# Raw token rows with their scale as a last column feed the expert gather, staged outside the tenth weight slot, whose load is asked for at the start of the phase

## The reference

```
xt      = rms_norm(h, norm_m[layer])                 # x * 1/sqrt(mean(x*x) + eps) * gain
group   = argmax softmax(xt @ w_rg + b_rg)           # 1 of 4 groups
experts = top 2 of the 8 experts of that group       # from xt @ w_re + b_re
hid     = silu(xt @ w_gate[e]) * (xt @ w_up[e])      # 1024 -> 512, for each chosen expert
h       = h + sum over the 2 experts of gate * (hid @ w_down[e])
```

## Time and profile before

| | us |
|---|---|
| runs, median of 3 | 1522.3 |
| the profiled execution, its own time | 1519.33 |
| its span in the profile | 1517.4 |
| TensorE busy | 1470.7 (97%) |
| VectorE busy | 634.6 (42%) |
| ScalarE busy | 285.0 (19%) |
| GpSimd busy | 73.0 (5%) |
| moved by DMA | 484.54 MB |

### The profile page before, as it was taken

The page is one execution under the profiler, slowest core; times in us unless marked ns, Lnnn a source line. Parts: engine busy times, 40 slices in busy tenths (PEclk is TensorE's granted clock), DMA queues, the critical chain, the costliest instruction groups (busy, mean ns, idle before and its releaser), DMA issues. The chain is left out here.

```text
span 1517.4 us, 20326 instructions
## 1 busy us (share of the span) xinstructions
PE 1470.7 (97%) x7727; PEld 738.4 (49%) x7727; DVE 634.6 (42%) x1657; ACT 285.0 (19%) x746; POOL 73.0 (5%) x123
## 2 busy tenths in 40 slices
PE   9999999999999999999999998899999999999995
PEld 8787878667333333333334445657333333333331
DVE  3666566445323323224244235735232322433324
ACT  2424244214110101001001004523010100110101
POOL 0101010001000000000000000001000000000000
PEclk9999999999999999999999999999999999999998
DMA  7432324467999999999999036785999999999993
GB/s 232 137 116 75 116 78 143 187 230 308 417 430 431 428 429 433 430 428 426 426 427 368 19 126 257 268 343 204 412 429 431 430 429 431 431 430 426 427 426 157
DMA packets 101504, 484.54 MB, mean 319 GB/s; under 512 B 16410, under 2 KB 51134, under 8 KB 67634
## 3 DMA queue, kind: packets, MB, share of 16 engines
q1 hardware_dynamic: 96818, 478.90, 78.0%
q0 software_dynamic: 4320, 4.42, 0.8%
q10 hardware_dynamic: 288, 0.14, 0.0%
HBM read 483.77 MB, written 10.97 MB: 326 GB/s over the span
## 5 line engine op out<-in xcount | busy, mean ns | idle before, releaser
L2539 PE MATMUL moe_ps_gate<-slots,moe_xrT 128*64 128x512 f32 x1024 | 228.1, 596 | 8.5 <-DMA slots<-in_w_gate_e_dram 8.5
L2539 PE MATMUL moe_ps_up<-slots,moe_xrT 128*64 128x512 f32 x1024 | 226.8, 595 | 0.0
L2566 PE MATMUL moe_ps_y<-slots,router_inputs 128*64 128x512 f32 x960 | 212.6, 595 | 0.0
L2412 DVE TENSOR_TENSOR resid<-resid,moe_ps_x 128x512 f32<-128x512 f32 x60 | 41.3, 688 | 252.7 <-PE moe_ps_x L2582 252.7
L2539 PEld LDWEIGHTS moe_ps_up<-slots,moe_xrT 128*64 128x64 f32 x1024 | 71.2, 137 | 150.9 <-issue 138.7
L2539 PEld LDWEIGHTS moe_ps_gate<-slots,moe_xrT 128*64 128x64 f32 x1024 | 72.2, 137 | 137.9 <-issue 136.7
L966 PE MATMUL gdn_bank<-gdn_xT,slots 128*128 128x288 f32 x512 | 136.3, 410 | 0.7 <-ACT slots L485 0.7
L2566 PEld LDWEIGHTS moe_ps_y<-slots,router_inputs 128*64 128x64 f32 x960 | 66.3, 137 | 124.9 <-issue 124.6
L2203 ACT ACTIVATE moe_xrT<-moe_ps_x,router_inputs 128x128 f32<-128x128 f32 x128 | 36.5, 367 | 379.1 <-PE moe_ps_x L2520 363.5
L966 PEld LDWEIGHTS gdn_bank<-gdn_xT,slots 128*128 128x128 f32 x512 | 92.6, 190 | 22.8 <-issue 1.1
L2381 DVE TENSOR_TENSOR router_inputs<-router_inputs,moe_ps_up 128x512 f32<-128x512 f32 x32 | 22.0, 688 | 195.0 <-PE moe_ps_up L2539 195.0
(11 more groups left out here) (509 smaller groups left out, 1817.9 us busy)
## 6 DMA issues: line engine op xcount, KB each, us to landing
slots<-in_w_gate_e_dram SPq DMA_DIRECT2D x40, 2048.0 KB, 23.0
slots<-in_w_up_e_dram SPq DMA_DIRECT2D x40, 2048.0 KB, 22.8
slots<-in_w_down_e_dram SPq DMA_DIRECT2D x40, 2048.0 KB, 25.8
slots<-in_w_gate_e_dram SPq DMA_DIRECT2D x48, 1024.0 KB, 26.2
slots<-in_w_up_e_dram SPq DMA_DIRECT2D x48, 1024.0 KB, 26.6
slots<-in_w_down_e_dram SPq DMA_DIRECT2D x48, 1024.0 KB, 26.0
slots<-in_w_in_a_dram SPq DMA_DIRECT2D x16, 1024.0 KB, 5.8
slots<-in_w_kv_dram SPq DMA_DIRECT2D x4, 2048.0 KB, 20.6
```

Source lines behind the costliest of these rows:

```text
L2412: V.tensor_tensor(half, half, banks[i][:, :], ALU.add).then_inc(s["summed"], 1)
L2539: last = T.matmul(ps[64 * e:64 * e + 64, :], xgT[:, k, 64 * e:64 * e + 64], slots[:, slot[2 * n + e], 512 * k:512 * k + 512], start=(k == ...
L2566: last = T.matmul(ps_y[64 * e:64 * e + 64, h, :], hidT[:, k, 64 * e:64 * e + 64], slots[:, slot[4 + e], 1024 * k + 512 * h:1024 * k + 512 ...
```

## The change

Rows are no longer normalised ahead of the gather. ACT reorders the raw rows into three buffers outside the slots: `norm_b`, `y_sb` and, for the 32 sample rows, the first 1024 columns of `xrT`, the last only after the logits have been made. SP stores them to `x_rows` in HBM, whose rows have 1025 numbers, and then stores `rstd` as the last column with three further DMAs. A gather brings 1025 numbers a row; GpSimd waits for it at once and copies the last column to `rcur` after the product of the group before. The scale is applied later: in `silu` as its `scale`, and in DVE's product with the up half, which becomes a `scalar_tensor_tensor`. For group 0 the scale goes into `sel0`, whose building instruction gets a second operation. The tail of the sample tile needs no clearing, since TensorE reads 32 rows of it. Piece 9 is the first DMA of the phase in layer 0, and follows pieces 4 and 5 in layer 1. ACT, DVE, GpSimd and SP wait for all six stores (`xn_stored` at 96) before the buffers are written again. The core of the diff:

```diff
@@ memory
-        sb("late_slots", [128, SLOT_COUNT - 7, SLOT_COLS])
-        xn = sb("last_slot", [128, SLOT_COLS])[:, 0:NT * D_MODEL].rearrange("p (t d) -> p t d", t=NT)
+        sb("late_slots", [128, SLOT_COUNT - 6, SLOT_COLS])
+        low = sb("low", [128, SLOTS])
+        rcur = sb("rcur", [128, 1])
...
+        xg_row = xr_flat[:, 0:D_MODEL + 1]
+        sel0 = xr_flat[:, 1544:1544 + NT * 128].rearrange("p (t r) -> p t r", t=NT)
+        x_rows = [norm_b[:, :], y_sb[:, :], xr_flat[0:T_DEC, 0:D_MODEL]]
@@ SP
             if layer:
                 m["prefetch"](sp, layer, (4, 5))
+            m["prefetch"](sp, layer, (9,))
             for t in range(NT):
-                sp.wait_ge(s["normed"], t + 1)
-                sp.dma_start(xn_dram[128 * t:128 * t + rows[t], :], xn[0:rows[t], t, :]).then_inc(s["xn_stored"], 16)
+                sp.wait_ge(s["turned_rows"], t + 1)
+                sp.dma_start(x_dram[128 * t:128 * t + rows[t], 0:D_MODEL], x_rows[t]).then_inc(s["xn_stored"], 16)
+            sp.wait_ge(s["inverse"], 1)
+            for t in range(NT):
+                sp.dma_start(x_dram[128 * t:128 * t + rows[t], D_MODEL:D_MODEL + 1], rstd[0:rows[t], t:t + 1], allow_slow_non_contiguous=True).then_inc(s["xn_stored"], 16)
             if layer == 0:
                 m["attn_inputs"](sp)
-            sp.wait_ge(s["xn_stored"], 16 * NT)
-            sp.wait_ge(s["gx_T"], 1)
-            m["prefetch"](sp, layer, (9,))
+            sp.wait_ge(s["xn_stored"], 16 * 2 * NT)
@@ POOL
-            P.memset(xn[32:64, 2, :], 0.0).then_inc(s["tail_cleared"], 1)
-            pool.wait_ge(s["tail_cleared"], 1)
-            P.memset(xn[64:128, 2, :], 0.0).then_inc(s["tail_cleared"], 1)
-            pool.wait_ge(s["tail_cleared"], 2)
-            pool.wait_ge(s["logits_made"], NT)
-            P.memset(xg, 0.0).then_inc(s["cleared"], 1)
+            pool.wait_ge(s["xn_stored"], 16 * 2 * NT)
+            pool.wait_ge(s["gx_T"], 1)
+            P.memset(xg_row, 0.0).then_inc(s["cleared"], 1)
...
+                pool.wait_ge(s["gathered"], n * 16)
+                pool.wait_ge(s["hidden"], n)
+                pool.sem_inc(s["waits_held"], 1)
+                P.tensor_copy(rcur[:, :], xg_row[:, D_MODEL:D_MODEL + 1]).then_inc(s["r_kept"], 1)
@@ ACT
-            act.wait_ge(s["inverse"], 1)
             for t in range(NT):
-                A.activation(by_tile(xn[0:r, t, :]), strided(resid[0:r, t, :]), ACT.Copy, scale=rstd[0:r, t:t + 1]).then_inc(s["normed"], 1)
+                if t == 2:
+                    act.wait_ge(s["logits_made"], NT)
+                A.copy(by_tile(x_rows[t]), strided(resid[0:rows[t], t, :])).then_inc(s["turned_rows"], 1)
...
+                    act.wait_ge(s["r_kept"], g)
+                    A.activation(hid, ps_gate[:], ACT.Silu, scale=rcur[:, 0:1]).then_inc(s["silued"], 1)
...
+            act.wait_ge(s["xn_stored"], 16 * 2 * NT)
             rows_kept(0)
             silu(0)
@@ DVE
-                    last = V.tensor_scalar(sel0[:, t, SLOTS * e:SLOTS * e + SLOTS], low, pos0[:, t, e:e + 1], None, ALU.is_equal)
+                    last = V.tensor_scalar(sel0[:, t, SLOTS * e:SLOTS * e + SLOTS], low[:, :], pos0[:, t, e:e + 1], rstd[:, t:t + 1], ALU.is_equal, ALU.mult)
...
+                    V.scalar_tensor_tensor(hid, hid, rcur[:, 0:1], ps_up[:], ALU.mult, ALU.mult).then_inc(s["hidden"], 1)
...
+            dve.wait_ge(s["xn_stored"], 16 * 2 * NT)
             overflow()
@@ PE
-            pe.wait_ge(s["normed"], NT)
-            pe.wait_ge(s["tail_cleared"], 2)
+            pe.wait_ge(s["turned_rows"], NT)
...
-                    last = T.matmul(ps_x[:, k // 4, k % 4, :], by_tile(xn[:, t, :])[:, k, :], sel0[:, t, :], start=(t == 0), stop=(t == NT - 1))
+                    last = T.matmul(ps_x[:, k // 4, k % 4, :], by_tile(x_rows[t])[:, k, :], sel0[0:rows[t], t, :], start=(t == 0), stop=(t == NT - 1))
```

More of the change, by code:

```diff
@@ L2007, in moe_phase @@
         place_o = y_sb[:, 0:TOP_K * NT * 128].rearrange("p (k t r) -> p k t r", k=TOP_K, t=NT)
[L2008 to L2009 removed]
         BELOW = -1024.0
         xr_flat = xrT[:].rearrange("p k r -> p (k r)")
[L2012 to L2014 removed]
+        xg_row = xr_flat[:, 0:D_MODEL + 1]
+        xg = xr_flat[:, 0:D_MODEL]
+        xgT = xr_flat[:, 1032:2056].rearrange("p (k r) -> p k r", k=KT)
+        obf = y_sb[0:1, 768:768 + 2 * OVER_GROUPS * N_EXPERTS].rearrange("p (b e) -> p b e", e=N_EXPERTS)
         selT = w_router.rearrange("p k n -> p (k n)")[:, 0:T_ALL]
+        sel0 = xr_flat[:, 1544:1544 + NT * 128].rearrange("p (t r) -> p t r", t=NT)
+        x_rows = [norm_b[:, :], y_sb[:, :], xr_flat[0:T_DEC, 0:D_MODEL]]
         hid = norm_b[:, 0:512]
@@ L2054, in moe_phase @@
         HALF = SLOT_COLS // 2
-        xn_dram = m["xn_dram"]
+        x_dram = m["x_dram"]
         W = m["expert_views"][layer]
@@ L2186, in _ @@
                 r = rows[t]
-                A.activation(xn[0:r, t, :], resid[0:r, t, :], ACT.Square, accum_out=ss[0:r, t:t + 1]).then_inc(s["squares"], 1)
+                if t == 2:
+                    act.wait_ge(s["squares"], 1)
+                A.activation(x_rows[t % 2][0:r, :], resid[0:r, t, :], ACT.Square, accum_out=ss[0:r, t:t + 1]).then_inc(s["squares"], 1)
             act.wait_ge(s["squares"], NT)
             A.activation(rstd[:, :], ss[:, :], ACT.Sqrt, scale=1.0 / D_MODEL, bias=m["eps"][:, 0:1]).then_inc(s["roots"], 1)
-            act.wait_ge(s["inverse"], 1)
             for t in range(NT):
-                r = rows[t]
-                A.activation(by_tile(xn[0:r, t, :]), strided(resid[0:r, t, :]), ACT.Copy, scale=rstd[0:r, t:t + 1]).then_inc(s["normed"], 1)
+                if t == 2:
+                    act.wait_ge(s["logits_made"], NT)
+                A.copy(by_tile(x_rows[t]), strided(resid[0:rows[t], t, :])).then_inc(s["turned_rows"], 1)
             act.wait_ge(s["gdiff"], 1)
@@ L2208, in silu @@
                 act.wait_ge(s["gate_made"], g + 1)
-                A.activation(hid, ps_gate[:], ACT.Silu).then_inc(s["silued"], 1)
+                if isinstance(g, int) and g == 0:
+                    A.activation(hid, ps_gate[:], ACT.Silu).then_inc(s["silued"], 1)
+                else:
+                    act.wait_ge(s["r_kept"], g)
+                    A.activation(hid, ps_gate[:], ACT.Silu, scale=rcur[:, 0:1]).then_inc(s["silued"], 1)
             def sel_kept(g, src):
@@ L2260, in _ @@
                     V.tensor_copy(xrT[:, 4 * j:4 * j + 4, at[t]], ps_xT[t][:, j, :, 0:rows[t]]).then_inc(s["xT_kept"], 1)
-            link(V.tensor_scalar(low, m["lanes"][:, 0:SLOTS], BELOW, None, ALU.add))
+            link(V.tensor_scalar(low[:, :], m["lanes"][:, 0:SLOTS], BELOW, None, ALU.add))
             dve.wait_ge(s["roots"], 1)
@@ L2380, in hidden @@
                 dve.wait_ge(s["silued"], g + 1)
-                V.tensor_tensor(hid, hid, ps_up[:], ALU.mult).then_inc(s["hidden"], 1)
+                if isinstance(g, int) and g == 0:
+                    V.tensor_tensor(hid, hid, ps_up[:], ALU.mult).then_inc(s["hidden"], 1)
+                else:
+                    V.scalar_tensor_tensor(hid, hid, rcur[:, 0:1], ps_up[:], ALU.mult, ALU.mult).then_inc(s["hidden"], 1)
             def turned(g):
```

9 lines of the change are left out of this document (3 added, 6 removed).

## The result

The changed kernel takes 1545.1 us, the median of four runs (1537.7 to 1549.8), beside 1522.1 for the kernel before (four runs, 1521.6 to 1524.0). The ratio is 1.014, with a 95% interval of 1.0123 to 1.0157: slower by 23 us, far above the range of the forecast, 1518.6 to 1524.8. The profiled execution took 1549.78 us with a span of 1547.8, which is 30.4 us more than the span before.

A forecast was written before the change was run, and what follows sets the result against it. The weight stream was taken to bound layer ends, with the phase-start path releasing it. Terms -1.2 (piece 9), +0.4 (sel0), +0.1 (product of hid) sum to -0.7 us: 1521.6 us against the 1522.3 median, range 1518.6 to 1524.8.

The forecast's parts named there:

- Reordering and storing: Phase start: ACT's copies, removed tail clearings, the moved gather-target clearing and stores behind piece 9 were each costed at 0.
- Piece 9: Weight stream at phase start: early issue gains 0.6 us a layer at the first whole pair, bounds 0 and 1.3.
- the move of piece 9 gives nothing: Rival at phase start: the dry start binds wholly, no stream gain, 1523.1 us; chance 0.23.
- the other two: Second halves of pieces 10 and 11, forecast to land 4.9 us after the first halves, at 1072.3.
- From the next pair on the queue stays full in both: Claim that the weight queue stays full after the first whole pair, with and without the change; total -1.2 us, both layers.
- the dip behind the pair: Sign: the stretch where the first whole weight pair starts shows a deeper dip than 295 GB/s.
- the waits for gate weights: Sign: TensorE's waits in the group loop fall from 8.5 to some 6 or 7 us; 5 would still fit.
- `sel0`: Ahead of group 0's product: second operation in six instructions adds 0.2 us a layer, 0.4 in all, upper bound 0.7.
- The stores: Phase start: row and column stores queue behind piece 9; costed at 0, with 3.6 us free behind 1054.8.
- deciding point: 1058.4: the time until which ACT can wait for the stores before TensorE stops in group 0's gate product.
- The rival's mechanism: Rival: column stores behind piece 9 land at 1060.9, stopping TensorE in the gate product; 1527.8 us, chance 0.11.
- In the group loop: DVE's product of `hid` costs 0.06 us more each, hidden except in the last group: 0.1 us; other terms 0.

The follow-up runs named there:

- e1: The changed kernel with the sample tile's tail cleared and TensorE reading 128 rows of it instead of 32; 1524.8 us, ratio 1.002.
- e2: The kernel before with only the third tile of group 0's product read at 32 rows instead of 128; 1539.9 us, ratio 1.0104.
- e5: The kernel before plus only the staging outside the slots and the early piece 9, all rows at 128; 1522.1 us, ratio 0.9999.
- e7: As e5, but only the first half of piece 9 issued early, the second after group 0's product; 1523.3 us, ratio 1.0001.
- e10: As e1, but sel0 built with one operation, so group 0's rows go unscaled; 1523.3 us, ratio 0.9998.
- e11: As e1, plus four filler products in TensorE's wait for sel0; 1522.7 us, ratio 0.9998.
- e6: As e1, but piece 9 issued after group 0's product, as in the kernel before; 1523.9 us, ratio 1.0009.
- e3: The changed kernel with the 32-row pairs of each half of group 0's product run together, 3 row-count changes, not 15; 1524.1 us, ratio 1.0015.
- e4: The changed kernel, alternating rows kept, plus eight filler products ahead of the wait for sel0; 1530.9 us, ratio 1.007.
- e9: As e4, but group 0's product ordered 32, 128, 128, 32 rows, two row-count changes; 1529.4 us, ratio 1.0041.
- e8: The kernel before with 10 instead of 26 filler products in the routing chain, 128 rows throughout group 0's product; 1527.5 us, ratio 1.0031.

## Why the prediction was wrong

**The step that failed** is "Reordering and storing", in its costs at 0. It costed the tail of the sample tile as two clearings on GpSimd that go, "beside this work: 0". That the same edit changes the form of 16 of TensorE's 48 instructions on the releasing path, from 128 rows to 32, was not named, not bounded and no rival. It stood in the diff (`sel0[0:rows[t], t, :]`), and the path through this product was called the one that counts. Its price at full clock is 2.8 us a layer, from 15 changes of 0.19. With the fallen clock, in the profiled execution, the product loses 9.4 and 8.8 us in the two layers, the table product 1.4 in each, and the gate product 3.0 and 2.0. Since nothing else can begin before that path is done, all of it reaches the end. e1 and e2 show it from both sides. What in the 32-row work holds the clock down stays open.

**Piece 9: forecast -0.6 us a layer, measured 0.** The rival "the move of piece 9 gives nothing" was right. The bound of 0 and its reason, a dry start, were in the working; the value between the bounds was a guess that the start is partly hidden. The failing term is that "the other two" land at 1072.3, 8.8 us after the last issue at 1063.5: in layer 1 of e5 it takes 9.9, beside 10.1 before. The forecast counts its gain at the first whole pair, and there e5 has one: in layer 1 the pair is in at 1072.2 + 13.9 = 1086.1, 52.0 us into the phase, where it was 53.1, in layer 0 0.1 us sooner. But it doesn't last, against the working's "From the next pair on the queue stays full in both". From the first transpose of layer 1 the last column, GB/s, has over 50 and 80 us, before and then in e5,

```profile
1032.88:1082.88 50.00, 49.33 (x333) 32.72 (x335) 27.33 (x119) 17.74 (x26) 5.95 (x8) 1.00 0.83 321
1032.88:1112.88 80.00, 79.33 (x472) 43.40 (x474) 36.58 (x139) 20.41 (x33) 7.33 (x11) 1.00 0.90 361
```

```profile
1034.14:1084.14 50.00, 49.33 (x331) 32.63 (x333) 27.62 (x119) 17.73 (x26) 6.07 (x8) 1.00 0.85 327
1034.14:1114.14 80.00, 79.33 (x470) 43.38 (x472) 36.86 (x139) 20.40 (x33) 7.45 (x11) 1.00 0.90 361
```

so e5 is 0.3 MB ahead after 50 us (0.7 us at 430 GB/s) and level after 80. What takes the lead back isn't shown. Its phases end at 471.05 and 469.89 us, where the kernel before has 469.72 and 470.00. Of the signs that were named, the early issue came, and the dip behind the pair (246 GB/s from 1073 to 1074 in e5); the waits for gate weights didn't fall to 6 or 7: they are 9.3 and 9.9 us in e5 and e7, and 8.3, 7.4 and 7.5 in e1, e10 and e11, whose longer product of `hid` is taken from them.

**`sel0`: forecast +0.2 us a layer, measured +0.36**, the upper bound. The six instructions in the kernel after, and with one operation in e10:

```profile
359.31 1.43 DVE L2317 TENSOR_SCALAR moe_xrT<-moe_low,moe_pos,moe_rstd 128x64 f32<-128x64 f32 x6
```

```profile
360.08 1.06 DVE L2322 TENSOR_SCALAR moe_xrT<-moe_low,moe_pos 128x64 f32<-128x64 f32 x6
```

It doesn't go with the width: 0.06 us an instruction at 64 columns as at 128. The step from 64 to 128 columns is the same for both forms, 1.27 - 1.07 and 1.63 - 1.43 = 0.20 us for six, so it is a fixed price of the second operation with its one number a row. The rule of the Trainium skill that the prediction weighed (VectorE: DVE Perf Modes, section "Mode 2×_2P — use both read ports for one tensor") is one on results a cycle, and these steps agree with it, both forms being equally fast for each further column; that the whole instruction would then take the same time doesn't follow from it, and isn't so.

**The stores: forecast 0, and 0 by luck of two kinds.** In the kernel after they land 9.4 to 12.2 us after their issue in layer 0, and the slow product hides them wholly; ACT's `rows_kept(0)` starts as it ends, at 376.02. In e11, where the product runs at full clock, the rows of TensorE and ACT in layer 1 are

```profile
1056.33 0.39 PE L2645 MATMUL moe_ps_x<-moe_xrT 128*128 128x128 f32 x2
...
1058.01 2.37 PE L2557 MATMUL moe_ps_gate<-slots,moe_xrT 128*64 128x512 f32 x10
```

```profile
1058.67 1.14 ACT L2212 ACTIVATE moe_xrT<-moe_ps_x,router_inputs 128x128 f32<-128x128 f32 x4 [10.07 <-DMA x_rows<-moe_rstd]
```

ACT is released by the column stores (landing 11.3 to 12.2 us after issue), 2 us after the product's end at 1056.7. The forecast's 1054.8 for the last row store was nearly right: it lands 22.3 us into the phase, 1055.2 in the forecast's times. But the last column store, to which it gave no time, lands at 24.3, which is 1057.2, 1.2 us before its deciding point of 1058.4. ACT's copy is wanted for the second half of the gate product, from 1058.01 + 3.5 = 1061.5, and ends at 1059.8, so TensorE isn't held. The rival's mechanism was there, and short of deciding by 1.7 us. With piece 9 issued late (e6) the last store lands at 18.3 us and ACT is released by TensorE, so it is that piece that pushes the stores back.

**In the group loop** the terms held. The new form of the product of `hid` (same groups view as the earlier trace rows) takes 748 ns, where 688 + 61 = 749 was forecast, and stays hidden:

```profile
L2393 DVE SCALAR_TENSOR_TENSOR router_inputs<-router_inputs,moe_rcur,moe_ps_up 128x512 f32<-128x512 f32 x30 | 22.4, 748 | 183.4 <-PE moe_ps_up L2552 183.4
```

The phases lose 0.4 and 0.6 us between the start of the up product of group 0 and their end. The forecast had 0.06 a layer there; e5, without the new form, has 1.2 and -0.3, so this is within what one execution scatters.

**The chances.** 0.12 was given to slower, 0.11 of it to the stores, which didn't decide. The named rivals covered queues and DVE, and none covered TensorE itself, the engine on the path.

## What to carry to other kernels

Compare the shape of every matrix instruction on the critical path before and after an edit, also where it only reads less: a 32-row tile among 128-row tiles saved nothing here and cost 0.19 us at each change, so try zeros as padding (e1, 0.2% from the kernel before), or at least put equal shapes together (e3, which still lost the clock in some executions). Where a stretch of TensorE stands near the fall of its clock (a short pause, fillers, small products), price the edit at both clocks and over several runs, since the clock's part, 11.0 and 9.4 us in the profiled execution, was over three times the edit's own 2.8. Asking for data earlier gained nothing here, since the next request then found the queue empty and paid the start that the early one had hidden: look what the next request will find.

## What the runs showed of the hardware that was not expected

- A change between 32 and 128 rows in a stream of float32 matrix instructions of 128 columns costs 0.19 us on the mean at 2.4 GHz (e3, e4, e9) and some 0.3 at 1.2 GHz: in the kernel after three pairs take 364.61 - 362.73 = 1.88 us; without changes, at the pitch of 0.43 in e3's layer 1, they would take 1.28.
- The same product at 1.2 GHz with the row count changing stayed there for 17 to 24 us, at 128 rows throughout for 3.4 to 6.8 (e6, e10, e8). In e9 the clock fell with no pause at all. Three changes (e3, 17.1 us) held it down as long as fifteen (e2, 17.1 and 20.5 us), so it isn't their number; how much 32-row work it takes stays open.
- Stores of 4 bytes a row to HBM, 288 in three issues, landed 9.4 to 11.9 us after issue in the kernel after, behind a 2 MB load, like the 4096-byte row stores beside them (9.5 to 14.2); in e6, with the load behind them, 3.7 to 6.2.
- A second operation with one number a row costs a float32 `tensor_scalar` on VectorE 0.06 us, at 64 columns as at 128 (the kernel after and e10; the earlier trace rows).
